# A decoder step on one core: the norm of the input projection moved to its copy-out, feed-forward groups written out, and a decode stage with smaller buffers

## The reference, cut to what matters

```python
z = rms_norm(x, norm_mix) @ w_in          # y = x * rsqrt(mean(x*x) + eps) * g
# differential attention over prompt columns, and for the 8 samples over
# cache_k[page_table], cache_v[page_table]: 32 pages of 128 positions each
s = q . k * HEAD_DIM_A**-0.5 + bias
a = softmax(s1) - lam * softmax(s2);  out = a @ v
# mLSTM heads, output norms
x = x + concat(a, m) @ w_out
x = x + square(relu(rms_norm(x, norm_ffn) @ w_up)) @ w_down
```

## Time and profile before

| | us |
|---|---|
| median of 3 runs (lowest, highest) | 4118.6 (4117.08, 4120.52) |
| the profiled execution | 4118.78 |
| its span, first to last instruction | 4117.1 |
| TensorE busy, matmuls | 3708.9 (90%) |
| VectorE busy | 1846.1 (45%) |
| ScalarE busy | 1283.7 (31%) |
| GpSimd busy | 717.0 (17%) |
| DMA moved | 574.47 MB, 140 GB/s over the span |

### The profile page before, as it was taken

The page is one execution under the profiler, slowest core; times in us unless marked ns, Lnnn a source line. Parts: engine busy times, 40 slices in busy tenths (PEclk is TensorE's granted clock), DMA queues, the critical chain, the costliest instruction groups (busy, mean ns, idle before and its releaser), DMA issues. The chain is left out here.

```text
span 4117.1 us, 66973 instructions
## 1 busy us (share of the span) xinstructions
PE 3708.9 (90%) x26528; PEld 3429.3 (83%) x26528; DVE 1846.1 (45%) x2885; ACT 1283.7 (31%) x1852; POOL 717.0 (17%) x436
## 2 busy tenths in 40 slices
PE   5999996676777999999995999999999999999998
PEld 4999996355666777777772898999999999999998
DVE  5222222595535676666665424333333333333333
ACT  2111111243103777777773213111221122111221
POOL 0000000000001777777774000000000000000000
PEclk8999998887867999999997999999999999999999
DMA  5434430414545888888884332222222222222221
GB/s 148 110 104 113 108 104 29 171 48 141 128 135 183 311 298 299 307 296 298 304 293 136 117 91 72 83 86 88 82 82 85 88 82 82 83 91 82 82 82 64
DMA packets 459413, 574.47 MB, mean 140 GB/s; under 512 B 38150, under 2 KB 333108, under 8 KB 458156
## 3 DMA queue, kind: packets, MB, share of 16 engines
q1 hardware_dynamic: 459260, 572.54, 44.3%
HBM read 521.68 MB, written 50.80 MB: 139 GB/s over the span
## 5 line engine op out<-in xcount | busy, mean ns | idle before, releaser
L1637 POOL TENSOR_TENSOR dc_vl<-dc_vpages,dc_vh 128x1024 fp32r<-128x1024 f32 x256 | 609.2, 2383 | 88.6 <-ACT dc_vh L1970 82.1
L67 PE MATMUL f_acc<-hidden_hi,ffn_lo 128*128 128x280 f32 x2048 | 603.1, 294 | 11.2 <-DVE hidden_lo L2374 11.2
L67 PE MATMUL f_acc<-xf_hi,ffn_lo 128*128 128x280 f32 x2048 | 597.7, 292 | 1.2 <-DVE xf_lo L2404 0.6
L69 PE MATMUL f_acc<-hidden_hi,ffn_hi 128*128 128x280 f32 x2048 | 598.7, 292 | 0.0
L68 PE MATMUL f_acc<-hidden_lo,ffn_hi 128*128 128x280 f32 x2048 | 597.7, 292 | 0.0
L69 PE MATMUL f_acc<-xf_hi,ffn_hi 128*128 128x280 f32 x2048 | 595.4, 291 | 0.0
L68 PE MATMUL f_acc<-xf_lo,ffn_hi 128*128 128x280 f32 x2048 | 594.5, 290 | 0.0
L67 PE MATMUL z_acc<-xn_hi,win_lo 128*128 128x280 f32 x1536 | 451.1, 294 | 18.8 <-DVE xn_lo L232 18.8
L69 PE MATMUL z_acc<-xn_hi,win_hi 128*128 128x280 f32 x1536 | 450.9, 294 | 0.0
L68 PE MATMUL z_acc<-xn_lo,win_hi 128*128 128x280 f32 x1536 | 449.6, 293 | 0.0
L2343 ACT ACTIVATE ffn_hi<-ffn_raw 128x2048 fp32r<-128x2048 f32 x127 | 242.4, 1908 | 637.2 <-PE f_acc L69 637.2
(11 more groups left out here) (351 smaller groups left out, 6396.5 us busy)
## 6 DMA issues: line engine op xcount, KB each, us to landing
dc_kpages<-in_cache_k SPq DMA_DIRECT2D x256, 512.0 KB, 4.9
dc_vpages<-in_cache_v SPq DMA_DIRECT2D x256, 512.0 KB, 4.5
ffn_raw<-in_w_up SPq DMA_DIRECT2D x64, 1024.0 KB, 6.3
ffn_raw<-in_w_down SPq DMA_DIRECT2D x64, 1024.0 KB, 5.1
win_raw<-in_w_in SPq DMA_DIRECT2D x48, 1024.0 KB, 6.1
ffn_raw<-in_w_out SPq DMA_DIRECT2D x16, 1024.0 KB, 6.2
z_scratch<-z_out SPq DMA_DIRECT2D x48, 280.0 KB, 2.4
sm_c<-in_state_C SPq DMA_DIRECT2D x32, 256.0 KB, 4.7
```

Source lines behind the costliest of these rows:

```text
L67: nc.tensor.matmul(out, wlo, xhi, start=first, stop=False)
L69: return nc.tensor.matmul(out, whi, xhi, start=False, stop=last)
L1637: G.tensor_tensor(vl[:, m % VBUF, :], vring[:, m % RING, :], vh[:, m % VBUF, :].bitcast(F32), ALU.subtract).then_inc(vlo, 1)
```

## The change

Three parts. In the projection the rows arrive in four quarters of their width (2 KB pieces), behind the gain and weight tile 0; the two first row tiles have a buffer of their own. Blocks of x are split with the gain alone, tile 0 is interleaved with the transposes, the sums of squares are made on ScalarE by rows, and 1/rms is turned into a row on all partitions by five small matmuls and multiplied in at the copy-out. In the decode stage there is one pair of `kh`/`kl` buffers, two value pages and rings of three; scores are computed in their own slot, what follows moves one slot forward, and the two value pages of a slot are multiplied in two places. In the feed-forward stage TensorE's 16 groups are written out; the other engines keep their loops.

```diff
+        xfree = sb("x_rows", [P, 2, d.dm])
+        xrow = lambda t: xfree[0:d.tt, t, :] if t < 2 else flow.raw[0:d.tt, t, :] if t < GROUP else \
             zc[0:d.tt, :, :].rearrange("p j t -> p (j t)")[:, 0:d.dm]
         xt = sb("xt", [P, d.kc, d.t])
         gain = sb("norm_mix_cols", [P, d.kc])
-        norm = NormBuffers(nc, ctx, d, sems, "mix", sb("mix_sq", [P, 2, d.t]), acc[1])
+        square = sb("x_square", [P, d.dm // 2])
+        ssq = sb("x_ssq", [P, 2, d.nt])
+        inv, root = sb("x_inv", [P, d.nt]), sb("x_root", [P, d.nt])
+        diag = sb("x_inv_diag", [P, d.nt, d.tt])
+        rstd = sb("x_rstd", [P, d.t])
...
+        ORDER = [(0, 2), (0, 3), (0, 0), (0, 1), (1, 2), (1, 3), (0, 4), (1, 0), (1, 1), (1, 4)]
...
+            samples = a["x_sample"].rearrange("b s m -> (b s) m")
             head = d.tt - N_META
-            sp.dma_start(xrow(0)[0:N_META, :], a["meta_tokens"]).then_inc(rows_in, 16)
-            sp.dma_start(xrow(0)[N_META:d.tt, :], x[0:head, :]).then_inc(rows_in, 16)
-            for t in range(1, d.nt - 1):
-                r0 = head + (t - 1) * d.tt
-                sp.dma_start(xrow(t), x[r0:r0 + d.tt, :]).then_inc(rows_in, 16)
-            sp.dma_start(xrow(d.nt - 1)[0:n_last, :], x[d.seq - n_last:d.seq, :]).then_inc(rows_in, 16)
-            sp.dma_start(xrow(d.nt - 1)[n_last:d.tt, :], a["x_sample"].rearrange("b s m -> (b s) m")).then_inc(rows_in, 16)
             sp.dma_start(gain[:, :], a["norm_mix"][0].rearrange("(k p) -> p k", p=P),
                          allow_slow_non_contiguous=True).then_inc(gain_in, 16)
+            sp.dma_start(raw[0], w[:, :, 0:P]).then_inc(flow.landed[0], 16)
+            for q in range(4):
+                cs = slice(q * QUARTER * P, (q + 1) * QUARTER * P)
+                sp.dma_start(xrow(0)[0:N_META, cs], a["meta_tokens"][:, cs]).then_inc(rows_in[q], 16)
+                sp.dma_start(xrow(0)[N_META:d.tt, cs], x[0:head, cs]).then_inc(rows_in[q], 16)
+                for t in range(1, d.nt - 1):
+                    r0 = head + (t - 1) * d.tt
+                    sp.dma_start(xrow(t)[:, cs], x[r0:r0 + d.tt, cs]).then_inc(rows_in[q], 16)
+                sp.dma_start(xrow(d.nt - 1)[0:n_last, cs], x[d.seq - n_last:d.seq, cs]).then_inc(rows_in[q], 16)
+                sp.dma_start(xrow(d.nt - 1)[n_last:d.tt, cs], samples[:, cs]).then_inc(rows_in[q], 16)
+            sp.dma_start(raw[1], w[:, :, P:2 * P]).then_inc(flow.landed[1], 16)
             sp.wait_ge(turned_ready, d.kc)
-            for j in range(GROUP):
+            sp.wait_ge(ssq_made, ORDER.index((1, GROUP - 1)) + 1)
+            for j in range(2, GROUP):
                 sp.dma_start(raw[j], w[:, :, j * P:(j + 1) * P]).then_inc(flow.landed[j], 16)
-            sp.wait_ge(xt_ready, d.kc)
-            sp.wait_ge(xt_tail, d.kc)
+            sp.wait_ge(xt_ready, 2 * d.kc)
             sp.dma_start(xt_dram.rearrange("(k p) t -> p k t", p=P), xt[:, :, :]).then_inc(xt_stored, 16)
...
+            def evacuate(k):
                 act.wait_ge(turned_ready, k + 1)
-                nc.scalar.activation(xt[:, k, split:d.t], turned[k % 2][:, 1, 0:d.t - split], ACT.Copy).then_inc(xt_tail, 1)
-
-            def first_tiles():
-                for j in range(2):
-                    act.wait_ge(flow.landed[j], 16)
-                    leading(j)
-            norm_scalar(nc, act, d, norm, xhi, first_tiles)
+                nc.scalar.activation(xt[:, k, 0:split], turned[k % 2][:, 0, 0:split], ACT.Copy).then_inc(xt_ready, 1)
+                nc.scalar.activation(xt[:, k, split:d.t], turned[k % 2][:, 1, 0:d.t - split],
+                                     ACT.Copy).then_inc(xt_ready, 1)
+
+            def squares(first, last):
+                for n in range(first, last):
+                    h, t = ORDER[n]
+                    if n:
+                        act.wait_ge(ssq_made, n)
+                    nc.scalar.activation(square[0:d.tt, :], xrow(t)[:, h * d.dm // 2:(h + 1) * d.dm // 2], ACT.Square,
+                                         accum_out=ssq[0:d.tt, h, t:t + 1]).then_inc(ssq_made, 1)
+
+            act.wait_ge(flow.landed[0], 16)
+            leading(0)
+            for q in range(4):
+                for k in range(QUARTER * q, QUARTER * (q + 1)):
+                    evacuate(k)
+                if q in (1, 2):
+                    squares(2 * q - 2, 2 * q)
+            act.wait_ge(flow.landed[1], 16)
+            leading(1)
+            squares(4, len(ORDER))
+            act.wait_ge(meaned, 2)
+            nc.scalar.activation(root[0:d.tt, :], inv[0:d.tt, :], ACT.Sqrt).then_inc(rooted, 1)
...
         def dve_copy_out(dve, n, j, rows=P):
             dve.wait_ge(flow.used, n + 1)
             for h in range(2):
-                nc.vector.tensor_copy(zc[0:rows, j, h * d.half:(h + 1) * d.half],
-                                      acc[j % 2][h][0:rows, 0:d.half]).then_inc(copied, 1)
+                cols = slice(h * d.half, (h + 1) * d.half)
+                nc.vector.tensor_tensor(zc[0:rows, j, cols], acc[j % 2][h][0:rows, 0:d.half],
+                                        rstd[0:rows, cols], ALU.mult).then_inc(copied, 1)
...
+        def x_leading(dve, k):
+            dve.wait_ge(xt_ready, 2 * k + 2)
+            nc.vector.tensor_scalar(xhi[:, k, :], xt[:, k, :], gain[:, k:k + 1], None, ALU.mult).then_inc(x_hi, 1)
+
+        def x_trailing(dve, k):
+            dve.wait_ge(x_hi, k + 1)
+            nc.vector.scalar_tensor_tensor(xlo[:, k, :], xt[:, k, :], gain[:, k:k + 1],
+                                           xhi[:, k, :].bitcast(F32), ALU.mult, ALU.subtract).then_inc(x_lo, 1)
 
         @block.vector
         def _(dve):
+            trailing(dve, 0, 0)
+            dve.wait_ge(gain_in, 16)
             for k in range(d.kc):
-                dve.wait_ge(turned_ready, k + 1)
-                nc.vector.tensor_copy(xt[:, k, 0:split], turned[k % 2][:, 0, 0:split]).then_inc(xt_ready, 1)
-                if k >= 1:
-                    square(dve, k - 1)
-            square(dve, d.kc - 1)
-            dve.wait_ge(gain_in, 16)
-            norm_scale(nc, dve, d, norm, xt, gain, xhi, xlo, lambda: [trailing(dve, j, j) for j in range(2)])
+                x_leading(dve, k)
+                if k % QUARTER:
+                    x_trailing(dve, k - 1)
+                if k % QUARTER == QUARTER - 1:
+                    x_trailing(dve, k)
+            trailing(dve, 1, 1)
+            dve.wait_ge(ssq_made, 2 * d.nt)
+            nc.vector.tensor_tensor(inv[0:d.tt, :], ssq[0:d.tt, 0, :], ssq[0:d.tt, 1, :], ALU.add).then_inc(meaned, 1)
+            dve.wait_ge(meaned, 1)
+            nc.vector.tensor_scalar(inv[0:d.tt, :], inv[0:d.tt, :], 1.0 / d.dm, EPS, ALU.mult, ALU.add).then_inc(meaned, 1)
+            dve.wait_ge(rooted, 1)
+            nc.vector.reciprocal(inv[0:d.tt, :], root[0:d.tt, :]).then_inc(inverted, 1)
+            dve.wait_ge(inverted, 1)
+            for t in range(d.nt):
+                nc.vector.tensor_scalar(diag[0:d.tt, t, :], ident[0:d.tt, 0:d.tt], inv[0:d.tt, t:t + 1], None,
+                                        ALU.mult).then_inc(diag_made, 1)
+            dve.wait_ge(spread_made, 1)
+            nc.vector.tensor_copy(rstd[:, 0:split], turned[0][:, 0, 0:split]).then_inc(rstd_made, 1)
+            nc.vector.tensor_copy(rstd[:, split:d.t], turned[0][:, 1, 0:d.t - split]).then_inc(rstd_made, 1)
+            dve.wait_ge(rstd_made, 2)
...
+            def turn(k):
                 if k >= 2:
-                    pe.wait_ge(xt_ready, k - 1)
-                    pe.wait_ge(xt_tail, k - 1)
+                    pe.wait_ge(xt_ready, 2 * k - 2)
                 for t in range(d.nt):
                     out = turned[k % 2][:, t // 4, (t % 4) * d.tt:(t % 4 + 1) * d.tt]
                     mm = nc.tensor.transpose(out, xrow(t)[:, k * P:(k + 1) * P], ident[0:d.tt, 0:d.tt])
                 mm.then_inc(turned_ready, 1)
-                if k >= 2:
-                    norm_mean(nc, pe, d, norm, k - 2)
-            for k in range(d.kc - 2, d.kc):
-                norm_mean(nc, pe, d, norm, k)
-            for j in range(2):
-                pe_tile(pe, j, j, hi[j], lo[j], first=True)
+
+            def first_tile(k):
+                if k == 0:
+                    pe.wait_ge(flow.lo_made, 1)
+                pe.wait_ge(x_lo, k + 1)
+                for h in range(2):
+                    cols = slice(h * d.half, (h + 1) * d.half)
+                    mm = exact_passes(nc, acc[0][h][:, 0:d.half], hi[0][:, k, :], lo[0][:, k, :],
+                                      xhi[:, k, cols], xlo[:, k, cols], k == 0, k == d.kc - 1)
+                if k == d.kc - 1:
+                    mm.then_inc(flow.used, 1)
+
+            for q in range(4):
+                pe.wait_ge(rows_in[q], 16 * (d.nt + 2))
+                for k in range(QUARTER * q, QUARTER * (q + 1)):
+                    turn(k)
+                    if q:
+                        first_tile(k - QUARTER)
```

(80 more changed lines are left out.)

99 lines of the change are left out of this document (21 added, 78 removed).

## The result

The changed kernel took 4165.4 us (median of 4 runs, 4159.6 to 4169.2) beside 4119.6 us of the kernel before on the same chip: ratio 1.011, with a 95% interval of 1.0093 to 1.0128. It is slower by 45.8 us where 19.4 were forecast (4138 against 4118.6). The profiled execution took 4168.2 us, its span 4166.5.

What follows compares the result with a forecast made beforehand. TensorE was taken to bound the projection and feed-forward stage, waits the decode stage, where no engine or queue is full. The terms: 4118.8 - 50 (projection) + 0 (feed-forward) + 69 (decode) = 4138 us, range 4090 to 4172.

Steps and rivals of the forecast that it cites:

- Projection, -50 forecast: Input projection: TensorE starts on raw x blocks, tile 1 done at about 60 us against 110.4; -50 us, bounds -42 to -56.
- Feed-forward, 0: Feed-forward stage: writing out TensorE's groups changes nothing, as the loop's turn costs nothing and code fetch is hidden; 0 us.
- Decode, +69 forecast: Decode stage: the new order closes one chain in every slot, mean interval 7.52 us with values; +69 us.
- four kinds of slot: Decode stage: ordinary slot 6.82 us, slot with exponentials 8.07, the two that turn probabilities 7.2 each.
- what comes once per sample: Decode stage: 0.20 us per interval kept from the kernel before, 6.90 against a mean of 6.70.
- upper bound of +100: Decode stage: the loss if every slot took 0.2 us more than forecast; the lower bound was +35.
- The single key pair: Decode stage: with one kh/kl pair, ScalarE may not write the next pair's kh before the current scores are through.
- Rival B: Decode stage: exponentials stay outside the chain; decode +32, total 4101 us, or 4066 if 6.90 holds; chances 0.15 and 0.07.
- A: Whole kernel: the summed forecast of 4138 us, with its errors between 4105 and 4170; chance 0.62.
- C: Decode stage: a ring of three lands the second value page a microsecond late per slot, 120 us more, 4258; chance 0.06.
- D: Projection: only half the gain, as VectorE's reciprocal chain or late tile 4 holds tile 2; 4163 us, chance 0.06.
- E: Feed-forward: unrolling shows, 15 stalls of 0.70 us saved (4128) or 0.70 of code fetch per group (4149); chance 0.04 together.

Runs made afterwards that it cites:

- e1: The changed kernel with the decode stage of the kernel before put back: 4073.3 us, ratio 0.9887.
- e2: The kernel before with only the new decode stage put in: 4214.4 us, ratio 1.0226.
- e3: The changed kernel with TensorE's hardware loop put back in the feed-forward stage: 4168.6 us, ratio 1.011.
- e7: The changed kernel with ten unused identity transposes on TensorE before the scores of each slot with exponentials: 4151.8 us, ratio 1.0078.
- e4: The changed kernel with ScalarE's exponentials moved behind the last key copies of their slot: 4115.4 us, ratio 0.9988.
- e12: The changed kernel with late exponentials (e4), three value pages (e5) and the mixers' mask in PSUM, products still tensor_scalar: 4091.9 us, ratio 0.9931.
- e5: The changed kernel with three buffers for rounded value pages instead of two, rings of three kept: 4157.7 us, ratio 1.0093.
- e8: The changed kernel with two kh/kl buffer pairs again, order of work kept: 4167.4 us, ratio 1.0115.
- e6: The changed kernel with rings of four pages, two rounded value pages kept: 4166.1 us, ratio 1.012.
- e10: The changed kernel with late exponentials (e4), three value pages (e5) and mixer products by scalar_tensor_tensor (e9): 4132.2 us, ratio 1.0026.
- e9: The changed kernel with three value pages (e5) and the four mixer products made by scalar_tensor_tensor instead of tensor_scalar: 4156.1 us, ratio 1.0077.

## Why the prediction was wrong in size and right in sign

**Projection, -50 forecast: right.** Tile 1 ended at 58.4 us (forecast 60), worth 52.0 there and 47.6 over the whole program (e1). Part of the rest went in a later stage of small matmuls. Its windows before and after:

```profile
1149.00:1266.00 117.00, 96.42 (x444) 87.75 (x444) 50.07 (x160) 1.70 (x8) 0.57 (x3) 0.66 0.47 148
```
```profile
1095.00:1218.00 123.00, 102.31 (x444) 93.31 (x444) 50.30 (x161) 1.70 (x8) 0.57 (x3) 0.62 0.45 140
```

The same 444 matmuls were busy 6 us longer at a granted clock of 0.62 instead of 0.66. From its first instruction to that of the decode stage it took 120.9 us before and 121.2 in e2, which has the old projection; in the changed kernel it took 127.9, in the other runs with the new one 123.4 to 128.4. Why the clock fell more often there was not tried and stays open.

**Feed-forward, 0: right.** e3 differs by 3 us, less than the runs can tell, and the stretch is the same to 1 us. The rule on branches in the Trainium skill (Runtime: NRT & Kernel Launch, Instruction fetch mechanics), which the prediction weighed and set aside, would have made e3 slower by 15 stalls; neither 0.13 us at the boundary nor e3 shows any.

**Decode, +69 forecast, +93 measured (e2): the term that was mis-sized.** In the changed kernel the stage takes 97.8 us more than before (1043.8 against 946.0 from the start of its first instruction to that of its last), 28.8 above the forecast. They come apart so:
- 17.3 us: eleven slots in which TensorE ran at 1.2 GHz. The forecast priced the idle time that the exponentials make at its own length, 1.25 us, and took every matmul after it at the duration that it had before. This is the step that failed. e7 took it away (16.8 us from first to last, 13.6 by the medians).
- 4.5 us: the first seven intervals were 50.8 us for 7 x 6.6. The first two sets of scores ran at the lower clock too (8.92 and 8.14 us against 6.73 for the next), which makes 3.6. It is the same omission, but not the same gap: TensorE came into the stage at the lower clock, without any exponentials.
- 2.5 and 1.7 us: the drain at the end cost 4.5 for 2, the earlier start gave 3.3 for 5.
- 2.7 us: all the other intervals, mean 7.54 for 7.52.

So the failed step put the clock at nothing, and it cost 17.3 + 3.6 = 20.9 us. An estimate from these rows: without them the decode stage would have cost 77 us for the 69 forecast and the kernel would have taken about 4145 us. The trace of before could have warned. In its decode stage, too, the clock fell three times amid work; the first time behind a gap of 1.29 us, in this window of it:

```profile
1475.50:1478.50 3.00, 3.00 (x15) 3.00 (x16) 1.62 (x4) 2.08 (x4) 2.56 (x2) 0.50 0.67 257
```

The rest of the stage was priced well, in part by luck. Of the four kinds of slot, 6.97, 8.09, 7.24 and 7.26 us were measured where 6.82, 8.07, 7.2 and 7.2 stood, 0.07 more in the mean; what comes once per sample was 0.15 where 0.20 was kept. The two errors nearly cancel. Luck, too, is that 97.8 lies under the upper bound of +100: that bound stood for 0.2 us more in every slot, not for a clock that falls in 13 of them.

**What the stage's loss consists of.** The distances from first to last part the 96.6 us between 878.3 and 974.9: 53.7 come with the exponentials' place (974.9 to 921.2 in e4), of which e7 took back the clock's 16.8; 22.1 with the second value page's wait (921.2 to 899.1 in e12, which has three pages and the mask in PSUM); 20.8 are left in e12. In an ordinary slot the value page's wait is only 0.23 of the 1.05 us lost (6.97 to 6.74 in e5, against 5.92 before). The other 0.82 no run removed. The first slots, which carry no values, show it as well: 5.31 us before (1298.00 to 1303.31) and 6.75 in the changed kernel (1278.06 to 1284.81), where TensorE waits for the kl of the pair that it has just turned, because the scores now stand in the pair's own slot. That this order is what costs there fits the rows; no run put the scores alone back, so it is argued and not shown.

One reason in the text was wrong without harm to the number. The single key pair, named there first as what closes the chain, costs nothing in the changed kernel (e8); whether it would in the shorter slots of e12 was not run. Rival B, exponentials outside the chain, did not occur, but its price was near: 4101 us stood, and e4, which makes B true, took 4115.

The sum: 4118.8 - 52.0 + 97.8 = 4164.6, and the profiled execution took 4168.2; the lower clock in the stage of small matmuls makes about the rest. Of the rivals, A is the one that the order of work bears out, and 4165 lies within its 4105 to 4170, near the upper edge, for a reason that A did not have. C and D did not occur: no page was late (e6), and the projection gave 47.6 of its 50 us. E did not either: both its cases would have shown in e3.

## What to carry to other kernels

When an edit makes a gap on TensorE, price two things: the gap, and the matmuls after it at the lower clock; look at the granted clock behind the longest gaps, in the trace of before already. On an engine that executes in order, ask of each instruction who waits for the next one: the same exponentials cost 50 us before the key copies, and behind them their slot is as long as an ordinary one. And judge a buffer count by which wait it lifts, with the instructions that then come to lie beside each other: added to e4, the third value page lost 17 us (e10), and gained 23 once GpSimd no longer held VectorE's products (e12).

## What the runs showed of the hardware that was not expected

- TensorE's granted clock fell from 1.00 to 0.50 after a gap of 1.94 to 1.97 us amid work at full clock, and not at once: the first matmuls of 1589.88 to about 1590.7 us ran at 0.28 us each, the later ones at 0.41. Of 30 such gaps (1.94 to 1.99 us) 11 had this effect, 19 did not. Their length alone does not decide it: these gaps are nearly equal, 30 gaps of 1.49 to 1.53 us in e5 had no such effect, and in the kernel before the clock fell behind one of 1.29 us and, twice, some 2.6 us after one of 1.0 us. What picks them is open.
- VectorE products with every operand in SBUF, 0.23 to 0.24 us each in the changed kernel when no GpSimd subtraction runs beside them, took up to 2.4 us beside one of 128x1024 (in e5 two of each four), whether written as tensor_scalar (e5) or as scalar_tensor_tensor (e9); with the mask in PSUM all 32 took 0.240 to 0.251 us (e12). The Trainium skill (SBUF — State Buffer, section "SBUF: two separate sides") says that VectorE and GpSimd share a port pair that one instruction holds for its whole length, and counts among VectorE's users of it those with two SBUF inputs against a GpSimd instruction that reads SBUF, besides its fast modes. All three runs agree with it. The tile rows of e5 and e12 (duration min/median/max ns):

```profile
L1896 DVE TENSOR_SCALAR dc_mixer<-dc_comb,dc_factor x32: 227/2368/2408, 1390.5 to 2243.6; 128x32 f32<-128x32 f32 x32
```
```profile
L1897 DVE TENSOR_SCALAR dc_mixer<-dc_comb,dc_factor x32: 240/243/251, 1384.4 to 2165.9; 128x32 f32<-128x32 f32 x32
```
